# Griffin-style gated layer on one core: the indexer's queries made by columns, for the 192 later rows only

## The reference, cut to what matters

```python
topk = min(TOPK_MAX, S // 4)                                    # 64
proj = jnp.einsum('bsd,dn->bsn', h, w_in[l])
qi = apply_rope(qi.reshape(B, S, IDX_HEADS, IDX_DIM), cos_i, sin_i)
ki = apply_rope(ki, cos_i, sin_i)
rel = jax.nn.relu(jnp.einsum('bqhd,bsd->bqhs', qi_b, ki))
score = jnp.einsum('bqhs,bqh->bqs', rel, wi_b)
score = jnp.where(causal[None], score, -jnp.inf)
_, sel = lax.top_k(score, topk)
```

## Time and profile before

| | |
|---|---|
| median of the runs | 798.16 us |
| the profiled execution, span | 796.4 us |
| PE, PE's weight loads, DVE, ACT, POOL busy | 792.7, 667.3, 481.5, 418.4, 46.8 us |
| DMA | 152.92 MB, 192 GB/s on average |

### The profile page before, as it was taken

The page is one execution under the profiler, slowest core; times in us unless marked ns, Lnnn a source line. Parts: engine busy times, 40 slices in busy tenths (PEclk is TensorE's granted clock), DMA queues, the critical chain, the costliest instruction groups (busy, mean ns, idle before and its releaser), DMA issues.

```text
span 796.4 us, 10773 instructions
## 1 busy us (share of the span) xinstructions
PE 792.7 (100%) x3810; PEld 667.3 (84%) x3810; DVE 481.5 (60%) x663; ACT 418.4 (53%) x670; POOL 46.8 (6%) x70
## 2 busy tenths in 40 slices
PE   9999999999999999999999999999999999999998
PEld 9998888888888888888888888888888888888887
DVE  7677766666677554668656455555455566665453
ACT  7574556665555454556465554555575444443431
POOL 4341000000000000000000000000000000000000
PEclk9999999999999999999999999999999999999999
DMA  9986665666666565666655665655665855555563
GB/s 316 313 264 198 186 187 168 183 199 180 199 187 187 171 194 162 196 189 193 177 154 173 166 176 161 185 160 172 173 185 182 293 195 184 185 194 189 187 194 122
DMA packets 81082, 152.92 MB, mean 192 GB/s; under 512 B 5136, under 2 KB 12944, under 8 KB 80784
## 3 DMA queue, kind: packets, MB, share of 16 engines
q1 hardware_dynamic: 80752, 152.06, 62.8%
q10 hardware_dynamic: 288, 0.30, 0.1%
HBM read 150.25 MB, written 2.10 MB: 191 GB/s over the span
## 4 chain that ended last, share of the span: by engine, by line
PE 97%; ACT 1%; DMA 1%; SPq 0%; issue 0%; DVE 0%; ACTq 0%
PE ps L527 30%; PE ps L529 30%; PE ps L528 29%; PE ps L538 2%; PE ps L569 1%; PE ps L580 1%; DMA raw<-in_w_in 1%; PE ps L638 0%; PE ps L749 0%; PE ps L748 0%; PE ps L747 0%; PE ps L646 0%; ACT L938 0%; ACT L832 0%; ACT g L832 0%; PE ps L626 0%
## 5 line engine op out<-in xcount | busy, mean ns | idle before, releaser
L1068 DVE TENSOR_TENSOR lo<-raw,hi 128x1024 fp32r<-128x1024 f32 (+2 forms) x279 | 335.2, 1204 | 290.2 <-ACT hi L819 288.4
L819 ACT ACTIVATE hi<-raw 128x1024 fp32r<-128x1024 f32 (+2 forms) x277 | 287.1, 1040 | 337.4 <-PE ps L529 323.8
L527 PE MATMUL ps<-hi,hT_hi 128*128 128x512 f32 (+2 forms) x936 | 364.3, 389 | 0.0
L529 PE MATMUL ps<-hi,hT_lo 128*128 128x512 f32 (+2 forms) x936 | 361.1, 386 | 0.0
L528 PE MATMUL ps<-lo,hT_hi 128*128 128x512 f32 (+2 forms) x936 | 360.8, 385 | 0.0
L529 PEld LDWEIGHTS ps<-hi,hT_lo 128*128 128x128 f32 x936 | 175.7, 188 | 35.1
L528 PEld LDWEIGHTS ps<-lo,hT_hi 128*128 128x128 f32 x936 | 175.8, 188 | 32.9
L527 PEld LDWEIGHTS ps<-hi,hT_hi 128*128 128x128 f32 x936 | 175.7, 188 | 33.0
L527 PE MATMUL ps<-hi,ogT_hi 128*128 128x512 f32 x128 | 50.1, 391 | 0.0
L529 PE MATMUL ps<-hi,ogT_lo 128*128 128x512 f32 x128 | 49.8, 389 | 0.0
L528 PE MATMUL ps<-lo,ogT_hi 128*128 128x512 f32 x128 | 49.8, 389 | 0.0
(11 more groups left out here) (167 smaller groups left out, 484.5 us busy)
## 6 DMA issues: line engine op xcount, KB each, us to landing
raw<-in_w_in SPq DMA_DIRECT2D x192, 512.0 KB, 3.8
raw<-in_w_out SPq DMA_DIRECT2D x32, 512.0 KB, 4.3
raw<-in_w_o_a SPq DMA_DIRECT2D x16, 512.0 KB, 3.7
raw<-in_w_o_b SPq DMA_DIRECT2D x16, 512.0 KB, 3.6
raw<-in_w_in SPq DMA_DIRECT2D x13, 384.0 KB, 5.3
raw<-in_w_in SPq DMA_DIRECT2D x8, 336.0 KB, 5.3
x_own<-in_x SPq DMA_DIRECT2D x4, 512.0 KB, 6.4
g<-in_x SPq DMA_DIRECT2D x1, 2048.0 KB, 10.3
```

Source lines behind the costliest of these rows:

```text
L527: mm(o, a_hi, w_hi[:, j], start=first and j == 0, stop=False)
L529: ins = mm(o, a_lo, w_hi[:, j], start=False, stop=j == 1 and last)
L819: activation(hi[:, slot, :, 0:width], raw[:, slot, :, 0:width], ACT.Copy).then_inc(hi_ready, 1)
L1068: tt(lo[:, slot, :, 0:width], raw[:, slot, :, 0:width], hi[:, slot, :, 0:width].bitcast(F32), ALU.subtract).then_inc(lo_ready, 1)
```

## The change

The query columns of `w_in` become the stationary operand, in blocks of 128, and the rows of x move, only the 192 rows from row 64 on: 16 units (`query_unit`), two chunks of 512 columns alternating from the first to the last unit. The result stands in columns, so nothing has to be transposed; the rotation is made in columns from transposed tables (`transpose_tables`, a swap of 32 partitions by ACT, `query_rope`). Key and head weights get their own 96 matmuls of 80 columns (`key_products`), with x stationary, 12 ahead of each unit of the second q chunk. The mean square comes from the x that is already there: ACT squares it (`square_x`), POOL adds eight tiles up, PE sums over the partitions (`sum_squares`). The chunk count falls by one (`C_QK` = 2), the first q chunk follows the queries, and loops of PE and DVE over chunks 3 to 10 are partly written out. The bias of rows 0 to 63 is cleared of the choice by one memset of DVE.

```diff
--- before.py
+++ after.py
-X_OWN_AFTER = ((1, 3), (1, 5), (1, 7), (2, 1))
...
-IDX_W = (384, 384, 256 + KIWI)
...
+Q_FIRST = TOPK
+Q_LATE = S - Q_FIRST
+QI_BLOCKS = IDX_HEADS * IDX_DIM // P // 2
...
+C_QK, C_V, C_G, C_M = 2, 10, 14, 18
-FIRST_UNITS = ((0, 0), (1, 0), (0, 1), (1, 1)) + tuple((c, i) for c in range(2) for i in range(2, CK))
-FIRST_END = CK + 2
...
+FIRST_UNITS = tuple((c, i) for i in range(CK) for c in range(2))
+FIRST_END = 2 * CK
+QI_COLS = (COL["qi"], COL["qi"] + CW)
+QI_BANKS = (2, 4)
...
-                if (c, i) in X_OWN_AFTER:
-                    load_x_own(X_OWN_AFTER.index((c, i)))
...
+                if u >= 2 * CK - 4:
+                    load_row(u - (2 * CK - 4))
+            for i in range(CK):
+                load(i % RING, 2 * CK + i, w_in, 2 * i, COL["qa"])
+                if i < 5:
+                    load_row(4 + i)
+                if i == 2:
+                    src = w_in[0][:, COL["kiwi"]:COL["kiwi"] + KIWI].rearrange("(k p) n -> p k n", p=P)
+                    sp.dma_start(kw[:, :, :], src).then_inc(kw_landed, 16)
...
+            for t in range(1, CK):
+                pool.wait_ge(x_squared, t + 1)
+                mark(tt(sq[:, 0, :], sq[:, 0, :], sq[:, t, :], ALU.add))
+                settle()
+            tt(sq[:, 0, 0:S], sq[:, 0, 0:S], sq[:, 0, S:2 * S], ALU.add).then_inc(x_summed, 1)
             pool.wait_ge(x_squares, 1)
             root(rstd, ms_x, ss_x, D, RT, NORM_EPS).then_inc(rstd_ready, 1)
...
+            def query_unit(u, i, eight):
+                def products(weights, moving, first=False, last=False):
+                    for j in range(2):
+                        for b in range(QI_BLOCKS):
+                            o = ps[:, QI_BANKS[eight] + b // 2, b % 2 * Q_LATE:(b % 2 + 1) * Q_LATE]
+                            ins = mm(o, weights[:, u % RING, j, b * P:(b + 1) * P], moving[:, 2 * i + j, Q_FIRST:S],
+                                     start=first and j == 0 and b % 2 == 0, stop=last and j == 1, skip_group_check=True)
+                    return ins
+                if u < EARLY:
+                    pe.wait_ge(hi_first, u + 1)
+                pe.wait_ge(hi_ready, u + 1)
+                if u == 0:
+                    pe.wait_ge(x_hi_first, 1)
+                    pe.wait_ge(x_lo_first, 1)
+                pe.wait_ge(split_hi, i + 1)
+                products(hi, hT_hi, first=i == 0)
+                pe.wait_ge(split_lo, i + 1)
+                products(hi, hT_lo)
+                if u == 0:
+                    pe.wait_ge(lo_first, 1)
+                pe.wait_ge(lo_ready, u + 1)
+                products(lo, hT_hi, last=i == CK - 1).then_inc(unit_done, 1)
...
+            def key_products(i):
+                if i == 0:
+                    pe.wait_ge(kw_lo_ready, 1)
+                    pe.wait_ge(tabT_ready, 1)
+                for k in (2 * i, 2 * i + 1):
                     for r in range(RT):
...
+                        a_hi, a_lo = (t[:, k, r * P:(r + 1) * P] for t in (hT_hi, hT_lo))
+                        o = ps[:, S0, r * P:r * P + KIWI]
+                        mm(o, a_hi, kw_hi[:, k, :], start=k == 0 and r == 0, stop=False, skip_group_check=True)
+                        mm(o, a_hi, kw_lo[:, k, :], start=False, stop=False, skip_group_check=True)
+                        ins = mm(o, a_lo, kw_hi[:, k, :], start=False, stop=k == KT - 1, skip_group_check=True)
+                if i == CK - 1:
+                    ins.then_inc(kw_done, 1)
...
+            def transpose_tables():
+                pe.wait_ge(ident_ready, 1)
+                pe.wait_ge(index_tables_ready, 3 * RT)
+                for n, table in enumerate((idx_cos_r, idx_sin_r)):
+                    for r in range(RT):
+                        o = ps[:, S0 + 1, n * S + r * P:n * S + (r + 1) * P]
+                        ins = nc.tensor.transpose(o.bitcast(F32R), table[:, r, :], ident_r[:, :])
+                ins.then_inc(tabT_psum, 1)
+            def sum_squares():
+                pe.wait_ge(x_summed, 1)
+                pe.wait_ge(tabT_ready, 1)
+                for r in range(RT):
+                    ins = mm(ps[:, S0 + 1, 2 * r:2 * r + 2], sq[:, 0, r * P:(r + 1) * P], ones, start=True, stop=True)
+                ins.then_inc(x_sums_psum, 1)
...
+                if i == 0:
+                    if isinstance(c, int) and c == C_QK + 1:
+                        pe.wait_ge(qi_read, 1)
+                    else:
...
             for u, (c, i) in enumerate(FIRST_UNITS):
-                if u < FIRST_END:
-                    early_unit(u)
-                else:
-                    unit(u, u % RING, 2 * i, hT_hi, hT_lo, chunk_bank(1), False, i == CK - 1, IDX_W[1])
...
+                if u == 11:
+                    transpose_tables()
+                query_unit(u, i, c)
+            for i in range(CK):
+                if i == 2:
+                    sum_squares()
+                unit(C_QK * CK + i, i % RING, 2 * i, hT_hi, hT_lo, chunk_bank(C_QK), i == 0, i == CK - 1)
...
+            for c in range(C_QK + 1, C_QK + 4):
...
+                    if c == C_QK + 1:
+                        key_products(i)
+                    if (c, i) == (C_QK + 3, 2):
+                        transpose_index_key()
...
+            def swap_queries(eight, quarter):
...
+                other = quarter ^ 1
+                if quarter == 0:
+                    act.wait_ge(unit_done, FIRST_END - 1 + eight)
+                    if eight > 0:
+                        act.wait_ge(qi_roped, eight)
+                to = qi_swap[quarter * 32:quarter * 32 + 32, :, :].rearrange("p (a b) s -> p a (b s)", a=2)
+                bank = QI_BANKS[eight]
+                activation(to, ps[other * 32:other * 32 + 32, bank:bank + 2, 0:2 * Q_LATE],
+                           ACT.Copy).then_inc(qi_swapped, 1)
...
+                if u == 11:
                     act.wait_ge(reduced, 1)
...
+                if i == CK - RING:
+                    act.wait_ge(tabT_psum, 1)
+                    activation(idx_tabT[:, :, :], ps[:, S0 + 1, :].rearrange("p (n s) -> p n s", n=2),
+                               ACT.Copy).then_inc(tabT_ready, 1)
...
+                    if c == C_QK and i == 3:
+                        act.wait_ge(x_sums_psum, 1)
+                        activation(ss_x, ps[:, S0 + 1, 0:4:2], ACT.Copy).then_inc(x_squares, 1)
+                    if c in (C_QK, C_QK + 1) and i < 4:
+                        swap_queries(c - C_QK, i)
+                    if c in (C_QK, C_QK + 1) and i == 6:
+                        queries_hi(c - C_QK)
+                    if (c, i) == (C_QK, 6):
+                        act.wait_ge(kw_landed, 16)
+                        activation(kw_hi[:, :, :], kw[:, :, :], ACT.Copy).then_inc(kw_hi_ready, 1)
+                    if (c, i) == (C_QK + 1, 0):
                         act.wait_ge(rstd_ready, 1)
...
+                    if (c, i) == (C_QK + 2, 2):
+                        key_out()
+                    if (c, i) == (C_QK + 3, 3):
+                        key_T_out()
...
+                    dve.wait_ge(tabT_ready, 1)
+                    dve.wait_ge(x_summed, 1)
+                    dve.wait_ge(qi_swapped, 4 * eight + 4)
+                    for a in range(2):
+                        four = ps[:, bank + a, 0:2 * Q_LATE].rearrange("p (b s) -> p b s", b=2)
+                        mark(tt(quads[0][:, a], four, cos_T.to_broadcast([P, 2, Q_LATE]), ALU.mult))
+                elif step == 1:
+                    settle()
+                    tt(qi_swap[:, :, :], qi_swap[:, :, :], sin_T.to_broadcast([P, QI_BLOCKS, Q_LATE]),
+                       ALU.mult).then_inc(qi_read, 1)
...
+                    if c in (C_QK, C_QK + 1) and 4 <= i <= 5:
+                        for step in ((0, 1), (2,))[i - 4]:
+                            query_rope(c - C_QK, step)
+                    if c in (C_QK, C_QK + 1) and i == 7:
+                        query_rope(c - C_QK, 3)
+                    if (c, i) == (C_QK, 7):
+                        dve.wait_ge(kw_hi_ready, 1)
+                        tt(kw_lo[:, :, :], kw[:, :, :], kw_hi[:, :, :].bitcast(F32), ALU.subtract).then_inc(kw_lo_ready, 1)
+                    if c == C_QK + 2 and i in (5, 6):
+                        key_rope(i - 5)
+                    if (c, i) == (C_QK + 3, 4):
...
```

More of the change, by code:

```diff
@@ L286, in build_layer @@
         consts_landed = sem("consts_landed")
-        x_own_landed = [sem(f"x_own_landed_{r}") for r in range(RT)]
+        kw_landed = sem("kw_landed")
         raw_landed = [sem(f"raw_landed_{i}") for i in range(RING)]
@@ L516, in _, with unit @@
             mm = nc.tensor.matmul
-            def unit(u, slot, k0, s_hi, s_lo, bank, first, last, width=CW):
-                w_hi, w_lo = (t[:, slot, :, 0:width] for t in (hi, lo))
+            def unit(u, slot, k0, s_hi, s_lo, bank, first, last):
                 pe.wait_ge(lo_ready, u + 1)
@@ L564, in transpose_roped @@
                     pe.wait_ge(qkT_ready, n)
```

(23 more changed lines are left out.)

427 lines of the change are left out of this document (199 added, 228 removed).

## The result

The changed kernel takes **811.87 us**, the median of four runs (809.22 to 812.77), beside 797.97 us for the kernel before on the same chip: a ratio of 1.017, interval 1.0153 to 1.0188. That is slower, as forecast, but by 13.9 us instead of 5.1, and outside the range. The profiled run is the quickest of the four, 809.22 us with a span of 807.3.

The account below looks back on a forecast made before the run. TensorE's instruction stream was taken as the bound: -5.6 (queries) + 10.6 (keys) + 0.4 + 0.2 - 0.55 = +5.1 us on 796.4, a span of 801.5, plus 1.8 makes 803.3 us; range 801 to 809.

Parts of the forecast that it names:

- the pace: Query and key matmuls on TensorE: 110 ns each, set by the weight load; queries 5.6 us gained, keys 10.6 us lost.
- The rival in which the load hides: Load does not set the pace: 93 ns at 192 columns, 47 at 80, giving 791.9 us; chance 0.12.
- start: First query unit waits for both k-tiles, so TensorE's first product comes at 6.0 us (5.6 to 6.5) instead of 4.68.
- tables: Four table transposes ahead of the twelfth query unit: 0.4 us, with no wait, as copies end near 34 and PE comes at 35.0.
- POOL: POOL's sum of squares, needed by PE at 54.3 us, was expected to end between 44.5 and 59.5.
- the step of the key and head weights: Splitting these weights into hi and lo before the second q chunk: made one unit ahead, no wait put in the sum.
- that cover: The one-unit lead of the key and head weight split; without it PE would wait at most 3 us.
- the query rotation: ACT's four swaps and DVE's column rotation, falling one by one between units of 2.7 us with three units of slack.
- a slower matmul: Upper side of the range: one matmul of 120 ns instead of 110 adds 4.8 us.
- POOL's wait: Rival: PE waits for POOL's late sum of squares in the first q chunk, 0 to 5.2 us, up to 808.5; chance 0.08.

Follow-up runs that it names:

- e7_keys_third: e6_warm with two of the three key and head weight products left out, so 32 of 96 matmuls stay: 797.34 us, ratio 0.9992.
- e4_256: e6_warm with the queries of all 256 rows made, so 384 matmuls of 256 instead of 192 columns: 807.27 us.
- e15_look: Second repeat profile of the changed kernel with 14 instead of 9 warm-up matmuls and nothing else: 811.04 us.
- e1_keys_early: Changed kernel with the hi and lo split of the key and head weights made four units earlier on ACT and DVE: 805.01 us, ratio 1.0104.
- e5_128: e1_keys_early with two of three query products 128 instead of 192 columns wide: 844.39, 844.46, 844.83 and once 804.00 us.
- e6_warm: e1_keys_early with 14 instead of 9 warm-up matmuls: 804.52 us, ratio 1.0084.

## Why the prediction was wrong

**Right: the pace.** 110 ns was taken for a matmul below the width at which its load shows; 111 was measured at 192 columns and 112 at 80. The rival in which the load hides is refuted at 192 columns (a pace of 93 ns would have shown as a first q chunk near 42 us), at 80 by e7_keys_third, and by e4_256, which wasn't 27 but 7 ns dearer for each matmul. The Trainium skill, "TensorE: Matmul & The Clock Gate", "Back-to-back issue gap", has some 81 ns for a load and matmul of 128 columns; the products here disagree, 109 to 112 ns for 80 and 192 columns alike. Only transposes come near it, the table transposes of the changed kernel with 85 ns each:

```profile
35.60 0.34 PE L597 MATMUL ps<-ident_r,idx_cos_r 128*128 128x128 f32 x2
35.77 0.34 PE L597 MATMUL ps<-ident_r,idx_sin_r 128*128 128x128 f32 x2
35.94 1.10 PE L556 MATMUL ps<-hT_hi,hi 128*128 128x192 f32 x8
```

So 110 ns is the floor of the products, and not of every pair of load and matmul; why transposes are quicker is open. That the floor is the load's own time rests on the earlier trace rows: in every run each matmul has a load, so none shows a narrow product without one.

**Right: start, tables, POOL.** First product 5.89 for 6.0, first q chunk 49.39 for 48.9. POOL's sum ended at 50.13 in the profile, inside its bounds of 44.5 to 59.5, and PE came to its sum at 54.89, 4.8 us later. Each of the 512 wide adds took 1.86 us:

```profile
35.42 13.03 POOL L507 TENSOR_TENSOR sq<-sq 128x512 f32<-128x512 f32 x7
48.53 1.60 POOL L509 TENSOR_TENSOR sq<-sq 128x256 f32<-128x256 f32 x1
```

**Wrong: the step of the key and head weights.** It said that "Their `hi` and `lo` (1280 columns, some 1.3 and 1.7 us by rows 9) are made one unit ahead" and "If that cover went, PE would wait for at most these 3 us", and put 0 in the sum. The durations were right (1.26 and 1.48). Three things weren't. First, *ahead* was counted in units of the program, not along the chain: the split stood on two engines behind a wait of ACT for DVE and of DVE for ACT, while the query rotation had been costed by itself, as lying "one by one between units of 2.7 us, with three units of slack". The slack was there once, and both steps spent it in the same place, units 6 and 7 of the first q chunk. The wait was 3.6 us. Second, a busy POOL was allowed for in `make_lo` alone (1.34 us), and not in the rotation, which by the rows above ended 1.8 us later for POOL's tables. Third, the price of a wait is more than its length: behind it the clock was lower, for a loss of 1.7 us in the profiled run and 3.4 in e15_look. Wait and clock together are 5.3 us of the 5.8 that the profiled span lies above the forecast's 5.1, and e1_keys_early gives them back. The other 0.5 are the start of the q chunk.

**The range.** Its upper end, 809, came from a slower matmul or POOL's wait, and not from this one. The uncovered chain should have been a rival with a chance and a price of its own. With the 3 us the text had, it would have stood at 806.3; with the clock, 808.0 to 809.7. The median of 811.87 lies higher still: with the 0.6 us of start and keys, 3.6 of wait and 3.4 of clock the sum is 810.9, and the last 1 us, from the two highest runs, stays open.

## What to carry to other kernels

Below the width at which the columns outlast the load, here between 192 and 256, a product costs as much as its load, 110 ns (a transpose 85 to 92); count matmuls there, not columns, put the narrow operand on the stationary side, and merge products that share one. A step that is "one unit ahead" on two engines is ahead only if its whole chain is: write it out from the moment at which the ring lets it start, with DVE's durations beside a busy POOL, and put side work where the ring is full. A wait of TensorE costs more than its length: those of 2.4 and 3.5 us here had 1.7 to 3.4 us of lower clock behind them, one of 1.0 us had none.

## What the runs showed that I had not expected

- In e5_128 TensorE worked without a gap from 6.17 us on, on products 192 and 128 wide, and stayed at 1.2 GHz until some 91 us, behind the first 512 wide matmuls: 40 us in all. Two more runs took as long, the fourth did not, and no run did of the kernels whose query matmuls are all 192 wide or wider. Why the fourth rose early isn't settled, and whether a longer warm-up helps was not tried.
- The same wait costs the clock 1.7 us in one run and 3.4 in the next, and with five more warm-up matmuls the spread of four runs is 0.6 us (e6_warm) instead of 3.9 (e1_keys_early).
- DVE and POOL slow each other: `make_lo` took 1.76 us at 65.45 and 69.16, while POOL added its tables, and 1.23 at 72.04. The Trainium skill, "SBUF — State Buffer", "Who interferes with whom", says that a VectorE instruction with two inputs in SBUF and a GpSimd one that reads SBUF shut each other out for a whole instruction. The rows of 65 to 71 us agree: each of POOL's adds that runs into one of DVE's ends some 0.6 us after it (67.81 after 67.21, 68.68 after 68.10, 69.83 after 69.23, 71.52 after 70.92).
